# Decoder layer in split float32 with seven-product matmuls: early reload of two quarters, and a turned weight ring

## The reference

```python
def hybrid_mixer(xn, conv_hist, w_in, sgu_ln_g, sgu_ln_b, w_s, b_s, conv_w, w_a_out, w_b_out, w_o):
    z = jnp.einsum("btd,dc->btc", xn, w_in)
    u, v, b_gate, c_gate, x_in, r_a, r_b = jnp.split(z, SPLITS, axis=-1)
    u = jax.nn.gelu(u)
    v = layer_norm(jax.nn.gelu(v), sgu_ln_g, sgu_ln_b)
    y_a = jnp.einsum("btc,cd->btd", u * chunk_spatial_mix(v, w_s, b_s), w_a_out)
    c_in = c_gate * x_in
    xp = jnp.concatenate([conv_hist.astype(c_in.dtype), c_in], axis=1)
    y_b = jnp.einsum("btc,cd->btd", b_gate * short_conv(xp, conv_w), w_b_out)
    h = jax.nn.sigmoid(r_a) * y_a + jax.nn.sigmoid(r_b) * y_b
    return jnp.einsum("btd,de->bte", h, w_o), xp[:, -(CONV_W - 1):], v

def swiglu(x, w_gate, w_up, w_down):
    return jnp.einsum("btf,fd->btd", jax.nn.silu(x @ w_gate) * (x @ w_up), w_down)
# x = x + rms_norm(mixer(rms_norm(x))); x = x + rms_norm(swiglu(rms_norm(x)))
```

## The kernel before

| parts | weights |
|---|---|
| 0-3, 4-15, 16-23 | `w_in`: U; C, X, B in turn; the gates RA, RB |
| 24-27, 28-31 | `w_a_out`, `w_b_out` (plain) |
| 32-53 | `w_gate` and `w_up` in turn |
| 54-57, 58-61, 62-65 | `w_down`, first, second and last row block (`kps` is 3 instead of 4 in the last) |

## Time and profile before

### The profile page before, as it was taken

How to read it: one execution, slowest core, us unless ns; L and a number is a source line. 1 busy time by engine, 2 the same in 40 slices (tenths; PEclk the granted TensorE clock), 3 DMA queues, 4 the chain that set the end, 5 groups by cost and what they waited for, 6 DMA issues and landing times. The chain is left out here.

```text
span 1730.9 us, 30832 instructions
## 1 busy us (share of the span) xinstructions
PE 1632.1 (94%) x12892; PEld 1598.1 (92%) x12892; DVE 996.0 (58%) x1388; ACT 550.6 (32%) x857; POOL 664.7 (38%) x498
## 2 busy tenths in 40 slices
PE   8999899999999999999998999999999987999893
PEld 5889899999999999999997899999999987999783
DVE  7657657568654342234367875555444446395777
ACT  5222322222223342112433432223322233242543
POOL 1011444544444442323522264444444423435273
PEclk9999999999999999999998999999999998999996
DMA  6302011221233237222313222222222241323213
GB/s 236 112 25 74 25 50 35 89 78 48 72 98 106 99 105 246 92 84 72 109 50 122 98 74 80 74 80 81 80 90 83 74 156 65 122 75 108 66 68 147
DMA packets 140605, 157.77 MB, mean 91 GB/s; under 512 B 5996, under 2 KB 127732, under 8 KB 139444
## 3 DMA queue, kind: packets, MB, share of 16 engines
q1 hardware_dynamic: 131844, 151.54, 27.0%
q10 hardware_dynamic: 8624, 4.27, 0.8%
HBM read 118.73 MB, written 37.09 MB: 90 GB/s over the span
## 5 line engine op out<-in xcount | busy, mean ns | idle before, releaser
L357 PE MATMUL ps<-tp,ring_hi 128*128 128x258 f32 x7676 | 1263.1, 285 | 46.0 <-POOL ring_lo L921 10.0
L357 PEld LDWEIGHTS ps<-tp,ring_hi 128*128 128x128 f32 x7676 | 1078.3, 192 | 50.0 <-issue 43.2
L357 PE MATMUL ps<-tp,ring_lo 128*128 128x258 f32 x3838 | 799.3, 284 | 0.0
L357 PEld LDWEIGHTS ps<-tp,ring_lo 128*128 128x128 f32 x3838 | 610.8, 192 | 0.0
L921 POOL TENSOR_TENSOR ring_lo<-stage,ring_hi 128x512 fp32r<-128x512 f32 (+1 forms) x212 | 304.3, 1442 | 698.9 <-ACT ring_hi L1096 698.8
L921 POOL TENSOR_TENSOR ring_lo<-ring_f,ring_hi 128x512 fp32r<-128x512 f32 (+1 forms) x204 | 283.8, 1404 | 212.8 <-ACT ring_hi L1096 92.3
L1096 ACT ACTIVATE ring_hi<-ring_f 128x512 fp32r<-128x512 f32 (+1 forms) x204 | 127.3, 626 | 461.7 <-DVE ring_f L1572 158.4
L1096 ACT ACTIVATE ring_hi<-stage 128x512 fp32r<-128x512 f32 (+1 forms) x212 | 128.6, 618 | 217.0 <-PE ps L357 157.9
L1569 DVE TENSOR_TENSOR ring_f<-stage 128x512 f32<-128x512 f32 (+1 forms) x51 | 38.3, 751 | 199.4 <-PE ps L357 121.9
L357 PE MATMUL ps<-wv_hi_t,tp 128*128 128x512 f32 x256 | 71.7, 396 | 0.0
L1590 DVE TENSOR_TENSOR s_a<-ps,s_a 128x516 f32<-128x516 f32 (+1 forms) x52 | 35.6, 684 | 44.9 <-PE ps L357 44.1
(11 more groups left out here) (214 smaller groups left out, 1298.2 us busy)
## 6 DMA issues: line engine op xcount, KB each, us to landing
stage<-in_w_in SPq DMA_DIRECT2D x24, 1024.0 KB, 5.9
stage<-in_w_gate SPq DMA_DIRECT2D x11, 1024.0 KB, 6.2
stage<-in_w_up SPq DMA_DIRECT2D x11, 1024.0 KB, 5.4
hid_dram<-hq SPq DMA_DIRECT2D x40, 258.0 KB, 2.9
tp_f<-hid_dram SPq DMA_DIRECT2D x20, 516.0 KB, 7.8
stage<-in_w_down SPq DMA_DIRECT2D x8, 1024.0 KB, 5.5
ob_dram<-q SPq DMA_DIRECT2D x16, 258.0 KB, 2.9
ra_dram<-q SPq DMA_DIRECT2D x16, 258.0 KB, 2.2
```

The costliest lines, as they stand in the source:

```text
L357: ins = pe.matmul(o, w, xc, start=first and n == 0, stop=last and n == 2)
```

## The change

For `w_down` q1 is reloaded four or five parts ahead into slot 5, and its high part is made ahead; q3 is loaded into slot 2 (behind p4 instead of p5) and split from there to slot 7; the sums are formed in another way and order (slot 1 first, slot 2 in place), and the first sum stands behind `c11`. Seven-product parts outside 34 to 53 keep positions 0, 1, 2 in places 4, 5, 6 and positions 3 to 6 in places 0 to 3. Work of ACT and DVE around parts 1 and 2 and inside 54, 58 and 62 is reordered. The number of matmuls, DMAs, sums and splits is unchanged.

```diff
+TURNED = [4, 5, 6, 0, 1, 2, 3]
@@ used / freed
-    if pos >= 4:
-        return BASE[FIRST_RUN[b]]
     return done(run, max(i for i, n in enumerate(QORDER[b]) if n // 2 == pos // 2))
+def places(b):
+    return [0, 1, 2, 3] if b in QORDER else list(range(7)) if B_UP0 < b < B_D else TURNED
 def freed(b, pos):
+    place = places(b)[pos]
     if b == B_F + 2:
-        return used(B_F, pos) if pos < 4 else done(LAST_RUN[B_UP0], 3)
-    return used(b - 1, pos)
+        return used(B_F, place) if place < 4 else done(LAST_RUN[B_UP0], 3)
+    if b - 1 in QORDER and place >= 4:
+        return BASE[FIRST_RUN[b - 1]]
+    return used(b - 1, places(b - 1).index(place))
@@ PE, halves of parts 54, 58, 62
-                        half(r, i, PLAIN_BANK[i], lambda q: (t_lo, 8 * n + (1, 3, 2, 4)[q]))
+                        half(r, i, PLAIN_BANK[i], lambda q: (t_lo, 8 * n + (1, 4, 2, 3)[q]))
@@ SP
+            EARLY = (B_D - 5, B_D + 1, B_D + MP + 1)
...
-                    t_load(n, 1, t_in[1], 5, BASE[r], kp)
                     t_load(n, 0, t_in[0], 4, done(r, 0), kp)
                     t_load(n, 2, t_in[2], 6, done(r, 2), kp)
                 if spills:
                     spill_hidden(j, 0)
+                if last:
+                    t_load(n, 3, t_in[3], 2, done(r, 4), kp)
+                if spills:
                     spill_hidden(j, 1)
-                if last:
-                    t_load(n, 3, t_in[3], 7, done(r, 5), kp)
-                if spills:
                     spill_hidden(j, 2)
                 if last:
                     t_load(n, 2, t_again, 3, done(r, 6), kp)
                 if spills:
                     spill_hidden(j, 3)
+                if b in EARLY:
+                    n = EARLY.index(b)
+                    sp.wait_ge(hid_saved[1], 16 * (MP * (n + 1) if n < 2 else J))
+                    t_load(n, 1, t_in[1], 5, BASE[LAST_RUN[(B_UP0, B_D, B_D + MP)[n]] + 1], kps(B_D + MP * n))
@@ ACT, parts 1 and 2
             u_plain(1, 0, Z)
+            prepare(2, 0, 1)
+            tx_split(2)
             u_plain(1, 1, W)
-            prepare(2, 0, 2)
-            tx_split(2)
+            prepare(2, 1, 3)
             u_plain(1, 2, Y)
+            prepare(2, 3, 5)
             tx_split(3)
             u_plain(1, 3, X)
-            prepare(2, 2)
+            prepare(2, 5)
@@ ACT, t_begin; t_split(0, 5) now stands ahead of part 52's s1, t_split(1, 5), t_split(2, 5) behind parts 56, 60
                 s1(r)
-                prepare(nb, 0, 2)
                 t_split(n, 4)
-                prepare(nb, 2, 3)
+                prepare(nb, 0, 1)
+                t_split(n, 0)
+                prepare(nb, 1, 2)
                 t_split(n, 6)
-                prepare(nb, 3)
-                t_split(n, 5)
-                t_split(n, 0)
+                prepare(nb, 2)
@@ ACT, inside parts 54, 58, 62
-                    for i, s in enumerate((7, 2, 1, 3)):
+                    for i, s in enumerate((7, 1, 2, 3)):
                         t_split(kb, s)
...
-                        if i == 2:
-                            prepare(b + 1, 0, 2)
-                    prepare(b + 1, 2)
+                        if i == 0:
+                            prepare(b + 1, 0, 3)
+                        elif i == 2:
+                            prepare(b + 1, 3, 5)
+                    prepare(b + 1, 5)
@@ DVE, last part before a row block (parts 53, 57 and 61 alike)
+                c11(r + 1, hq[:, 0])
+                hidden(0, 0, c11_done)
                 if last:
                     t_total(0, 0, r + 1)
-                c11(r + 1, hq[:, 0])
-                hidden(0, 0, c11_done)
                 u1(r + 1)
@@ DVE, t_end
+                t_total(n, 1, r - 1)
+                t_rest(n, 7)
                 t_total(n, 2, r - 1)
-                t_total(n, 1, r - 1)
                 t_rest(n, 5)
                 down_add(r, 0)
-                t_rest(n, 7)
                 t_rest(n, 0)
+                sums(b + 1, 0)
                 down_add(r, 1)
                 t_total(n, 3, r - 1)
                 t_rest(n, 1)
                 down_add(r, 2)
-                sums(b + 1, 0)
+                sums(b + 1, 1)
+                sums(b + 1, 2)
                 t_rest(n, 2)
                 down_add(r, 3)
-                for i in range(1, 4):
-                    sums(b + 1, i)
+                sums(b + 1, 3)
                 t_rest(n, 3)
```

More of the change, by code:

```diff
@@ L230, in slot_rows, with ring @@
             return tp_f[s][:, part, 0].rearrange("p k c -> p (k c)")[:, 0:D]
[L232 to L233 removed]
+        def ring(t, b, pos, kp=MP):
+            return t[:, places(b)[pos], 0:128 * kp].rearrange("p (k c) -> p k c", c=128)
         def home(t):
@@ L265, in w_ring @@
             if b != B_UP0:
-                hi, lo = ring_hi[:, pos], ring_lo[:, pos]
+                hi, lo = ring_hi[:, places(b)[pos]], ring_lo[:, places(b)[pos]]
             elif pos < 3:
@@ L1345, in t_split @@
                 ks = slice(0, kps(B_D + MP * n))
-                if s in T_SUMS:
-                    act.wait_ge(t_sum, 4 * n + T_SUMS.index(s) + 1)
+                if s < 4:
+                    act.wait_ge(t_sum, 4 * n + s + 1)
                 else:
                     act.wait_ge(t_in[s - 4], 32 * (n + 1))
-                act.activation(slot(s, 0, both, ks), slot_f(s, 1, both, ks), ACT.Copy).then_inc(t_hi, 1)
+                if s == 7:
+                    act.wait_ge(prod_done, done(LAST_RUN[B_D + MP * n - 1], 5))
+                act.activation(slot(s, 0, both, ks), slot_f(2 if s == 7 else s, 1, both, ks), ACT.Copy).then_inc(t_hi, 1)
             def t_begin(n, r, nb):
                 s1(r)
-                prepare(nb, 0, 2)
                 t_split(n, 4)
-                prepare(nb, 2, 3)
+                prepare(nb, 0, 1)
+                t_split(n, 0)
+                prepare(nb, 1, 2)
                 t_split(n, 6)
-                prepare(nb, 3)
-                t_split(n, 5)
-                t_split(n, 0)
+                prepare(nb, 2)
             for j in range(1, J):
@@ L1659, in _ @@
             mix_evict(4, Z)
+            sums(2, 0)
+            u_plain(1, 1)
+            sums(2, 1)
+            sums(2, 2)
             tx_rest(1)
-            u_plain(1, 1)
-            sums(2, 0)
             u_plain(1, 2)
@@ L1666, in _ @@
             u_plain(1, 3)
-            sums(2, 1)
-            sums(2, 2)
             sums(2, 3)
@@ L1967, in t_rest @@
                 dve.wait_ge(t_hi, 8 * n + T_HI.index(s) + 1)
-                if s in T_SUMS:
-                    dve.wait_ge(t_sum, 4 * n + T_SUMS.index(s) + 1)
-                dve.tensor_tensor(slot(s, 1, both, ks), slot_f(s, 1, both, ks), slot_v(s, 0, both, ks), SUB).then_inc(t_lo, 1)
+                if s < 4:
+                    dve.wait_ge(t_sum, 4 * n + s + 1)
+                dve.tensor_tensor(slot(s, 1, both, ks), slot_f(2 if s == 7 else s, 1, both, ks), slot_v(s, 0, both, ks), SUB).then_inc(t_lo, 1)
             def t_total(n, s, run):
                 ks = slice(0, kps(B_D + MP * n))
-                x, y = {0: (5, 4), 2: (7, 5), 1: (7, 0), 3: (3, 1)}[s]
-                for src in {0: (1, 0), 2: (3, 1), 1: (3,), 3: ()}[s]:
-                    dve.wait_ge(t_in[src], 32 * (n + 1))
-                if s == 3:
-                    dve.wait_ge(t_again, 32 * (n + 1))
-                dve.wait_ge(prod_done, done(run, {0: 1, 2: 4, 1: 3, 3: 6}[s]))
+                x, y = ((5, 4), (2, 0), (2, 5), (3, 1))[s]
+                for counted in ((t_in[1], t_in[0]), (t_in[3],), (), (t_again,))[s]:
+                    dve.wait_ge(counted, 32 * (n + 1))
+                dve.wait_ge(prod_done, done(run, (1, 3, 4, 6)[s]))
                 if s in (1, 3):
-                    dve.wait_ge(t_sum, 4 * n + {1: 1, 3: 3}[s])
+                    dve.wait_ge(t_sum, 4 * n + s // 2 + 1)
                 dve.tensor_tensor(slot_f(s, 1, both, ks), slot_f(x, 1, both, ks), slot_f(y, 1, both, ks), SUB).then_inc(t_sum, 1)
@@ L2070, in down_rest @@
                 sums(nb, 0)
-                if n is not None:
-                    t_total(n, 0, r)
                 if count:
@@ L2077, in down_rest @@
                 gather(m, 0, s_b, gs, ready)
+                if n is not None:
+                    t_total(n, 0, r)
                 u1(r)
@@ L2123, in _ @@
                 sums(b + 1, 0)
+                c11(r, g[:, m, 0])
                 if last:
                     t_total(1, 0, r)
-                c11(r, g[:, m, 0])
                 u1(r)
```

23 lines of the change are left out of this document (13 added, 10 removed).

## The result

The changed kernel takes 1715.38 us (median of 4 runs, 1713.03 to 1716.08); the kernel before beside it takes 1732.51 (4 runs, 1729.63 to 1735.66). The ratio is 0.9896, 95% interval 0.9881 to 0.9912: 17 us are gone, where 28 were forecast. The profiled execution took 1716.08 us, its span is 1714.4, its mean granted clock 0.979.

What follows compares the result with a forecast made beforehand. PE is busy 94% of the span, so only its waits and low clock can be won. -7.7 + 8.7 - 12.7 - 5.9 - 10.5 = -28.1 from 1732.6 gives 1704.5 us, range 1696 to 1718.

Steps and rivals of the forecast that it cites:

- Rival 2: DVE and POOL delay each other at parts 58, 62 and 63, and the save lands late: 10.2 us more, 1714.7; chance 0.23.
- the save at its late end: Before part 54's third half, the last save lands at 1425.8 instead of 1421.5; counted as +4.3 us in rival 2.
- Part 23 to 24: Untouched by the diff; ACT waits for later products of part 23, so PE waits 3.0 and 2.9 us: +8.7 with clock.
- rival 1: Part 24 is cheap because ACT's late weights are covered: price 0 to 3 us instead of 8.7, say 1698; chance 0.15.
- Part 1 to 2: PE's 6.11 us wait for POOL's remainder of position 1 goes: -7.7 us, with 1.5 us to spare at position 3.
- 195.5 for the piece: In part 2, position 3's sum is done at 193.3 and its piece at 195.5; p3 needs it at 197.0.
- Parts 53 to 55: The waits at p5 and at part 55's p1 go; 9.1 of 21.8 us excess remains, so -12.7 us.
- six of some 0.7: DVE in part 53 from 1407.7: six operations of some 0.7 us and two of 2.25, so q2's remainder ends at 1416.5.
- The save: Part 54, before t_end: the last save takes 3.4 us, landing at 1421.5; the third half then waits 5.3 us.
- Parts 57 to 63: Parts 57 to 59 give -5.9 us; parts 61 to 63 give -10.5 us, with a 1.2 us wait left.
- 1.0 us to spare: Part 58's third half: DVE has q1's remainder at 1528.7 and PE needs it at 1529.7.

Runs made afterwards that it cites:

- Experiment 3: The changed kernel with part 24 in places 4, 5, 6, 0 and part 25 in 1, 2, 3, 4: 1704.18 us, ratio 0.9832 against the kernel before.
- experiment 7: The changed kernel with POOL's last two weight pieces (positions 2 and 3) moved behind the split of q3: one run, 1714.53 us.
- experiments 6: The changed kernel with q2's remainder in part 53 made ahead of two hidden products: 1717.35 us, ratio 0.9902 against the kernel before.
- third edit of 8: Part 2's fourth weight sum ahead of the third token sum's remainder, added to free places for parts 24, 25 and the later save wait: 1700.52 us together.

## Why the prediction was right, and where it fell short

The forecast was 1704.5, measured 1715.4: within the range, faster as forecast, 11 us short. Rival 2's 1714.7 is nearer, but partly by luck: of its 10.2 us the stretches at parts 58 and 63 came (1.5 each), while the save at its late end (4.3) and part 62 (3.7) nearly did not. What made up for them it had not priced: part 2's piece, the low clock in part 54's first half, and the clock behind unchanged waits. By its steps:

- **Part 23 to 24: right,** in mechanism and size (waits 3.08 and 2.58 against 3.0 and 2.9, together +9.3 against +8.7). ACT's queue shows it, with a piece of the weights that could go only when the product had ended, and `a_split(2)` behind it:

```profile
649.53 0.64 ACT L1105 ACTIVATE ring_hi<-stage 128x512 fp32r<-128x512 f32 x1 [4.77 <-PE ps L362]
650.06 0.62 ACT L1206 ACTIVATE q<-q 128x516 f32<-128x516 f32 x1
650.59 2.00 ACT L1201 ACTIVATE tp<-gv 128x1024 fp32r<-128x1024 f32 x2
```

  Experiment 3 confirms it by removal; rival 1 falls.
- **Part 1 to 2: the piece of position 3 mis-sized.** DVE began the sum at 193.9 and had it at 194.5, about 1 us behind the forecast's 193.3, since two mixer steps of 0.16 took 1.25 each beside POOL. "195.5 for the piece" left POOL 1.3 us for it. POOL started at 194.68, and two pieces took 5.07, of which the first, position 3's, had 3.8, beside DVE's remainder. PE waited 1.65 instead of having 1.5 to spare. By the same token p3 of part 63 waits 1.28, which rival 2 had.

```profile
194.68 5.07 POOL L930 TENSOR_TENSOR ring_lo<-ring_f,ring_hi 128x512 fp32r<-128x512 f32 x2 [1.44 <-DVE ring_f L1595]
```

- **Parts 53 to 55: right in kind, 2.7 short, nearly all in the first half.** `c11` at 1408.6, the landing of q0 and its sum came as forecast (all times here 7.1 later than before's). The step that failed is "six of some 0.7": two hidden products took 1.68 and 1.01 (1.3 us more together), so q2's remainder was done at 1424.5 instead of 1423.6. PE waited 2.52 instead of 1.5, and that wait brought a low clock (first row 1.20) which the forecast had not counted.
- **The save: 4.9 us, not 3.4.** The last one was issued at 1425.99 and DVE went on at 1431.07; the issue was 0.9 later than forecast as well.

```profile
1425.99 0.52 SPq L831 DMA_DIRECT2D hid_dram<-hq  x1
```

```profile
1431.07 2.85 DVE L1998 TENSOR_TENSOR tp_f<-tp_f,tp_f 128x2064 f32<-128x2064 f32 x1 [5.10 <-DMA hid_dram<-hq]
```

  It hardly lengthened the wait at the third half (5.74 against 5.3), as PE itself came 2.6 later. The estimate of 2.6 us from the Trainium skill (DMA: Bandwidth & Descriptors, "Anatomy of one DMA") is about half of what this save took behind a reload.
- **Parts 57 to 63: spares too thin.** "1.0 us to spare" at part 58 became a wait of 1.27, since of the four operations there a remainder took 3.39 and a sum 2.81 instead of 2.3. In part 62 the wait was 0.84 for 1.2.

```profile
1520.03 3.39 DVE L1988 TENSOR_TENSOR tp<-tp_f,tp 128x2064 fp32r<-128x2064 f32 x1
```

- **A cost that I did not count: the clock behind waits that the change leaves alone,** +3.6 us. I do not take it for the change's work: each of these waits costs more or less by where the low clock falls, and experiment 3, which has all of the change but the places of parts 24 and 25, stood 2.1 us below the kernel before around 920, level with it at part 28 and 2.0 above it around 1027. With one profiled execution of each this is argued, not shown.

What fits is the forecast and rival 2 in part: DVE and POOL get in each other's way at 2, 53, 58 and 63, and the save is late. The Trainium skill (SBUF, "SBUF: two separate sides") says that a DVE operation with two SBUF inputs and a GpSimd operation that reads SBUF exclude each other whole. The runs agree where the two were taken apart (0.70 against 1.68, experiment 7), and in the stretches of 1.1 us. Which of the two waits the traces show too; it stands in the last section.

My weak point was the judgement of the spare time. I wrote of rival 2 that POOL has few pieces while the four operations run; the meetings that mattered were at part 2, in part 53 ahead of them, and in part 58, where two of the four met a piece each. That the wait for the saves was needless I had not seen: it was in the code, and I took its place in the queue as given.

## What to carry to other kernels

When buffers are renumbered, list for every user of the ring what it now waits for, the parts that the diff leaves alone first: here one of them took back a third of the gain, and a table of two entries with one changed condition returned it. Price a saved wait by what its chain meets next, since three reorderings (experiments 6 and 7 and the third edit of 8) removed or shortened their wait and gave it back within a few stages; the two edits that lasted took a condition away (a place that was free, a save that nobody needed yet) instead of reordering the same work. Where spare time is worked out from single durations on DVE and POOL, take off a microsecond for each meeting on DVE's side, and more on POOL's (2.5 at part 2), before calling it spare.
